# HGRN rows multiplied by the root on GpSimd before they are stored, block decays taken by levels, and the weight splits placed in head 2

## What is computed

```python
hn = rms_norm(h, mix_norm[0])                  # h * rsqrt(mean(h^2) + eps) * gain
u, q_b, f_b, i_b, g_b = split(hn @ w_in_even)
y_a = s5_mixer(u, ...)                         # complex scan over tokens, GELU, GLU
y_b = hgrn2_mixer(q_b, f_b, i_b, g_b, ...)     # 4 heads of 128
h = h + concat(y_a, y_b) @ w_out_even
# in hgrn2_mixer: log_f from f_b, k = (1 - lb) * sigmoid(-f_b), b = cumsum(log_f)
# o = (q * exp(b)) S + causal(q, decay, k) v ; o = rms_norm per head * silu(g_b)
```

## Time and profile before

| | us |
|---|---|
| median of 3 runs | 2599.13 (2596.79 to 2599.51) |
| the profiled execution | 2594.84 |
| its span, first to last instruction | 2593.1 |
| TensorE busy in it | 2458.1 (95%) |
| VectorE busy | 1176.7 (45%) |
| ScalarE busy | 558.3 (22%) |
| GpSimd busy | 822.5 (32%) |
| mean granted TensorE clock | 0.975 of full |

### The profile page before, as it was taken

One profiled execution on the slowest core, in us unless ns is written; L12 is line 12 of the kernel. 1 busy time (PEld: TensorE's weight loads), 2 busy tenths in 40 slices (PEclk: granted clock), 3 DMA queues, 4 the chain that ended last, 5 costly groups with the idle time before them and its releaser, 6 DMA issues.

```text
span 2593.1 us, 32792 instructions
## 1 busy us (share of the span) xinstructions
PE 2458.1 (95%) x13062; PEld 1994.9 (77%) x13062; DVE 1176.7 (45%) x1170; ACT 558.3 (22%) x882; POOL 822.5 (32%) x493
## 2 busy tenths in 40 slices
PE   8999946899999999999996999989999999999997
PEld 6887835688888888888885776668888888888885
DVE  6886388432432422425517355652432332424625
ACT  3111435311001011011212145631001001011215
POOL 3422331132333333333331334552333333333320
PEclk9999967999999999999998999999999999999998
DMA  7372511211111111111213111021111111111211
GB/s 206 104 116 79 159 56 35 98 48 49 49 49 49 49 49 49 49 49 49 65 41 97 41 25 58 24 67 48 49 49 49 49 49 48 46 46 48 63 48 65
DMA packets 249160, 159.65 MB, mean 62 GB/s; under 512 B 32132, under 2 KB 236136, under 8 KB 249064
## 3 DMA queue, kind: packets, MB, share of 16 engines
q1 hardware_dynamic: 233944, 133.92, 18.0%
q10 hardware_dynamic: 15136, 24.58, 3.5%
HBM read 131.81 MB, written 25.49 MB: 61 GB/s over the span
## 4 chain that ended last, share of the span: by engine, by line
PE 85%; DVE 9%; ACT 3%; issue 2%; DMA 1%; POOL 0%; SPq 0%; ACTq 0%; POOLq 0%; DVEq 0%
PE ps L604 70%; PE ps L1086 3%; PE ps L758 2%; PE ps L1118 2%; PE ps L1046 1%; PE ps L1059 1%; PE ps L1070 1%; DVE hg_queries_keys L1861 1%; PE ps L671 1%; PE ps L779 1%; DVE stage L1538 1%; ACT x_hi L1169 1%; DVE hg_block_decay L1847 1%; PE ps L983 1%; DVE residual L2054 1%
## 5 line engine op out<-in xcount | busy, mean ns | idle before, releaser
L459 POOL CAST w_hi<-w_raw 128x1024 fp32r<-128x1024 f32 x198 | 217.9, 1100 | 1499.3 <-PE ps L604 1218.4
L604 PE MATMUL ps<-x_hi,w_hi 128*128 128x512 f32 x1600 | 496.9, 392 | 8.7 <-issue 4.2
L604 PE MATMUL ps<-x_hi,w_lo 128*128 128x512 f32 x1600 | 493.9, 390 | 0.0
L604 PE MATMUL ps<-x_lo,w_hi 128*128 128x512 f32 x1600 | 493.6, 390 | 0.0
L461 POOL TENSOR_TENSOR w_lo<-w_raw,w_hi 128x1024 fp32r<-128x1024 f32 x198 | 484.3, 2446 | 15.9
L604 PE MATMUL ps<-mid_hi,w_hi 128*128 128x512 f32 x1216 | 376.2, 391 | 8.7 <-DVE mid_lo L1913 5.8
L604 PE MATMUL ps<-mid_lo,w_hi 128*128 128x512 f32 x1216 | 375.3, 390 | 0.0
L604 PE MATMUL ps<-mid_hi,w_lo 128*128 128x512 f32 x1216 | 375.3, 390 | 0.0
L604 PEld LDWEIGHTS ps<-x_hi,w_hi 128*128 128x128 f32 x1600 | 300.2, 188 | 75.7 <-issue 9.9
L604 PEld LDWEIGHTS ps<-x_hi,w_lo 128*128 128x128 f32 x1600 | 301.0, 188 | 62.8
L604 PEld LDWEIGHTS ps<-x_lo,w_hi 128*128 128x128 f32 x1600 | 300.9, 188 | 62.9
(11 more groups left out here) (290 smaller groups left out, 2459.4 us busy)
## 6 DMA issues: line engine op xcount, KB each, us to landing
w_raw<-w_mlp_in_in SPq DMA_DIRECT2D x64, 512.0 KB, 4.0
w_raw<-w_mlp_out_in SPq DMA_DIRECT2D x64, 512.0 KB, 4.0
w_raw<-w_in_even_in SPq DMA_DIRECT2D x20, 512.0 KB, 4.2
residual_dram<-residual ACTq DMA_DIRECT2D x2, 4096.0 KB, 12.9
fqig_dram<-stage ACTq DMA_DIRECT2D x16, 512.0 KB, 2.7
w_raw<-w_ple_gate_in SPq DMA_DIRECT2D x16, 512.0 KB, 3.9
x_tokens<-x_in SPq DMA_DIRECT2D x8, 512.0 KB, 7.3
w_raw<-w_out_even_in SPq DMA_DIRECT2D x8, 512.0 KB, 4.2
```

The source lines that it names most:

```text
L459: pool.tensor_copy(WH[:, b, :], RAW[:, b, :]).then_inc(S["w_hi_done"], 1)
L604: ins = pe.matmul(acc[:, h, :], w[:, k, :], x[:, k0 + k, h * HALF:(h + 1) * HALF], start=(k == 0 and w is wh and x is xh), stop=(k == kts ...
```

## The change

GpSimd now multiplies each HGRN row tile by the root as it leaves the projection (`scale_unit`), behind the split of the slab two units later, and SyncE stores it (`spill`), between the loads of slabs. ScalarE only copies. The multiplications of f, q and gate in the heads, the scale per token of the values, its transposes and its column go. `head_load(hd)` waits for the stores of its own rows only. The block decays of head 0 are made one level at a time between its updates, and the clearing of two PSUM banks goes behind update 1. GpSimd splits output slabs 22 and 23 behind `gate_mult(2)` in place of ahead of `gate_mult(0)`.

```diff
 # SyncE
-            with sp.Fori(0, HEADS) as hd:
-                for j, c0 in enumerate((2 * S5W, S5W, 3 * S5W, 4 * S5W)):
-                    load(j % 2, hd * 4 + (4 + j - 1), cols(w_in, bass.ds(hd * P + c0, P)))
+            def head_slab(s):
+                hd, j = divmod(s - SLAB["heads"], 4)
+                c0 = (2 * S5W, S5W, 3 * S5W, 4 * S5W)[j] + hd * P
+                load(s % 2, s - 1, cols(w_in, slice(c0, c0 + P)))
+            def spill(u):
+                sp.wait_ge(S["hg_scaled"], u - 3)
+                sp.dma_start(fqig_dram[(u - 4) * P:(u - 3) * P, :], ST[u % 2][:, :]).then_inc(spilled[u % 2], 16)
...
+            for s in range(4, 8):
+                head_slab(s)
+            for u in range(4, 15):
+                spill(u)
+                head_slab(u + 4)
...
             tile_of_y(0)
-            for s in range(2):
...
-                load(s, 20 + s - 1, src)
-                tile_of_y(s + 1)
+            head_slab(19)
+            spill(15)
+            glu_slab(0)
+            tile_of_y(1)
+            spill(16)
+            glu_slab(1)
+            tile_of_y(2)
+            spill(17)
             tile_of_y(3)
...
+            spill(18)
             load(0, 21, cols(w, slice(0, P)))
-            for b in range(2):
-                sp.wait_ge(spilled[b], 16 * 10)
             sp.wait_ge(S["acc_done"], 20)
             def head_load(hd):
                 p = hd % 2
+                for b in range(2):
+                    sp.wait_ge(spilled[b], 16 * (4 + 2 * hd))
...
             head_load(0)
+            spill(19)
             load(1, 22, cols(w, slice(P, 2 * P)))
 # GpSimd
-            run(4, 4, 16)
-            one(20, 19)
-            one(21, 20)
...
+            def scale_unit(u):
+                if u == 4:
+                    pool.wait_ge(S["rstd_done"], 1)
+                pool.wait_ge(S["acc_free_act"], u - 3)
+                pool.tensor_tensor(ST[u % 2][:, :], ST[u % 2][:, :], RSTD[:, :], ALU.mult).then_inc(S["hg_scaled"], 1)
+            for s in range(4, 22):
+                one(s, s - 1)
+                if s >= 6:
+                    scale_unit(s - 2)
...
-            queries(0)
-            gate_scale(0)
-            one(22, 22)
-            one(23, 24)
             for hd in range(HEADS):
                 gate_mult(hd)
-                if hd < HEADS - 1:
-                    queries(hd + 1)
-                    gate_scale(hd + 1)
+                if hd == 2:
+                    one(22, 22)
+                    one(23, 24)
 # TensorE
-            pe.wait_ge(S["rstd_done"], 1)
-            for n in range(NB):
-                ins = pe.transpose(PS[:, 5, n * GRP:(n + 1) * GRP], RSTD[0:GRP, n * P:(n + 1) * P], ident[0:GRP, 0:GRP])
 # ScalarE
                 fn(ST[b][:, :], flat(ACC[b]), ACT.Copy).then_inc(S["acc_free_act"], 1)
-                act.wait_ge(S["acc_free_act"], u - 3)
-                act.dma_start(fqig_dram[(u - 4) * P:(u - 3) * P, :], ST[b][:, :]).then_inc(spilled[b], 16)
...
-                act.wait_ge(S["hg_z"], u + 1)
+                act.wait_ge(hg_loaded[p][half], 48 * (hd // 2 + 1))
...
-                act.wait_ge(S["hg_g_scaled"], hd + 1)
+                act.wait_ge(hg_g_loaded[hd % 2], 16 * (hd // 2 + 1))
...
-                for c in range(4):
-                    ins = fn(VT[:, half, c * P:(c + 1) * P], PS[:, (2, 3)[half], c * P:(c + 1) * P], ACT.Identity,
-                             scale=rstd_col[:, 4 * half + c:4 * half + c + 1])
-                told(ins, "hg_v_copied")
+                told(fn(VT[:, half, :], PS[:, (2, 3)[half], :], ACT.Copy), "hg_v_copied")
 # VectorE
-            own(dve.tensor_copy(rstd_col[:, :], PS[:, 5, 0:NB * GRP:GRP]))
...
-            def forget_in(hd, half):
-                f = FR[:, hd % 2, half, :]
-                dve.wait_ge(hg_loaded[hd % 2][half], 48 * (hd // 2 + 1))
-                told(tt(f, f, RSTD[:, half * HALF:(half + 1) * HALF], ALU.mult), "hg_z")
...
-            for half in range(2):
-                forget_in(0, half)
             z_low(3)
             near_masks()
             for half in range(2):
                 query_decay(0, half)
-            block_decays(0)
-            dve.wait_ge(S["glu_sig"], 2)
-            for half in range(2):
-                own(dve.memset(PS[:, (6, 7)[half], :], 0.0))
...
                     if hd == 0:
+                        for j in {3: (3, 4, 5, 6)}.get(l, (l,) if l < 3 else ()):
+                            block_decay(0, j)
+                        if l == 1:
+                            dve.wait_ge(S["glu_sig"], 2)
+                            for half in range(2):
+                                own(dve.memset(PS[:, (6, 7)[half], :], 0.0))
                         if l < 4:
                             glu_product(l)
...
-                    if nxt < HEADS and l == (1 if hd == 0 else 2):
-                        for half in range(2):
-                            forget_in(nxt, half)
                     if nxt < HEADS and l == 4:
-                        block_decays(nxt)
+                        for j in range(LEVELS):
+                            block_decay(nxt, j)
```

More of the change, by code:

```diff
@@ L122, in build @@
     eps = small("eps", [P, 1])
-    rstd_col = small("rstd_of_tokens", [P, NB])
     def col(name, i):
@@ L321, in _, with glu_slab @@
                 load(s % 2, s - 1, cols(w_in, slice(s * P, (s + 1) * P)))
-            with sp.Fori(0, HEADS) as hd:
-                for j, c0 in enumerate((2 * S5W, S5W, 3 * S5W, 4 * S5W)):
-                    load(j % 2, hd * 4 + (4 + j - 1), cols(w_in, bass.ds(hd * P + c0, P)))
+            def head_slab(s):
[5 more added lines that the diff above has]
+                sp.dma_start(fqig_dram[(u - 4) * P:(u - 3) * P, :], ST[u % 2][:, :]).then_inc(spilled[u % 2], 16)
+            def glu_slab(s):
+                src = a["s5_w_glu"][0][:, s * 256:(s + 1) * 256].rearrange("(k p) n -> p k n", p=P)
+                load(s, 20 + s - 1, src)
+            for s in range(4, 8):
[3 more added lines that the diff above has]
+                head_slab(u + 4)
             def tile_of_y(k):
@@ L499, in _ @@
                                pattern=[[16, 8], [0, 16]], channel_multiplier=-1).then_inc(S["full_masks"], 1)
-            run(4, 4, 16)
-            one(20, 19)
-            one(21, 20)
-            def queries(hd):
-                for half in range(2):
-                    q = QR[:, hd % 2, half, :]
-                    pool.wait_ge(hg_loaded[hd % 2][half], 48 * (hd // 2 + 1))
-                    pool.tensor_tensor(q, q, RSTD[:, half * HALF:(half + 1) * HALF], ALU.mult).then_inc(S["hg_q_scaled"], 1)
-            def gate_scale(hd):
-                pool.wait_ge(hg_g_loaded[hd % 2], 16 * (hd // 2 + 1))
-                pool.tensor_tensor(G[:, :], G[:, :], RSTD[:, :], ALU.mult).then_inc(S["hg_g_scaled"], 1)
+            def scale_unit(u):
[7 more added lines that the diff above has]
+                    scale_unit(s - 2)
             def gate_mult(hd):
@@ L1830, in query_decay @@
                 dve.wait_ge(S["hg_f_made"], u + 1)
-                dve.wait_ge(S["hg_q_scaled"], u + 1)
+                dve.wait_ge(hg_loaded[p][half], 48 * (hd // 2 + 1))
                 if hd >= 2:
@@ L1841, in blocks, with block_decay @@
                 return TT[:, hd % 2, o:o + (T >> l)]
-            def block_decays(hd):
-                dve.wait_ge(S["hg_f_made"], 2 * hd + 2)
-                for l in range(LEVELS):
-                    pairs = blocks(hd, l).rearrange("p (n two) -> p n two", two=2)
-                    ins = tt(blocks(hd, l + 1), pairs[:, :, 0], pairs[:, :, 1], ALU.mult)
-                    if l < LEVELS - 1:
-                        own(ins)
-                told(ins, "hg_blocks")
+            def block_decay(hd, l):
+                if l == 0:
+                    dve.wait_ge(S["hg_f_made"], 2 * hd + 2)
+                pairs = blocks(hd, l).rearrange("p (n two) -> p n two", two=2)
+                ins = tt(blocks(hd, l + 1), pairs[:, :, 0], pairs[:, :, 1], ALU.mult)
+                if l < LEVELS - 1:
+                    own(ins)
+                else:
+                    told(ins, "hg_blocks")
+                    dve.wait_ge(S["hg_blocks"], hd + 1)
             def update(hd, l):
```

9 lines of the change are left out of this document (3 added, 6 removed).

## The result

The changed kernel takes 2600.94 us (median of 20 runs, 2593.15 to 2608.97), the kernel before, beside it on the same chip, 2597.14 (20 runs, 2587.68 to 2600.3). The medians lie 3.8 us apart. The ratio estimated from all runs of both is 1.0022, its 95% interval 1.0011 to 1.0032: slower by 5.7 us, at the edge of the 0.2% that can be told. The forecast was 1.7 us slower. That the level forecast, 2600.8, is so near to the median measured is partly luck: it was built on a median of three runs, 2599.13, and twenty put the kernel before at 2597.14.

What follows compares the result with a forecast made beforehand. TensorE was taken to bound the kernel, so terms count only where it waits: for VectorE at S5 and in the heads. 15.3 + 1.5 - 10.2 - 3.5 - 1.4 = +1.7 us, 2600.8 us forecast median; range 2590 to 2609.

Steps and rivals of the forecast that it cites:

- A collision costs 2.08 us: Projection with S5: each added GpSimd multiplication that meets a VectorE operation with both operands in SBUF costs VectorE 2.08 us.
- rival (b): Projection: part is hidden, the memset takes one, small waits two, split 16 stays behind L1772; 8.3 us less, 2592.5; chance 0.17.
- The skip addition 9.4 us later: L1724 in the S5 part: seven multiplications, 14.6 us, less the 5.0 wait and 0.2 for the root column's copy.
- Behind it 5.9 us: From L1724 to the S5 output: multiplications of units 11 and 13, a cast and split 16, less 1.9, together +5.9 us.
- rival (a): Locks cost more: multiplications hold VectorE their whole 2.34 us in eleven places, units 4 to 14; 2607 us; chance 0.28.
- rival (c): No delay in S5: VectorE's multiply is not held or slack exists; only the heads' 15.1 us count, 2584; chance 0.05.
- The clock, one fall, 1.5 us: After TensorE's added waits in S5, one fall of the granted clock costs 1.5 us, bounds 0 to 8.5.
- The queues: nothing: Sixteen stores move from ScalarE to SyncE, with slab loads behind them; loads stay early enough and saved issues gain nothing.
- Head 0 shorter by 10.2 us: Head 0: first update 11.3 us earlier, then +2.0 in VectorE's queue and -0.9 for value copies; bounds 8 to 12.
- Head 1, 3.5 us: Head 1: shorter by 3.5 us (2.4 to 4.2), as f multiplications and ScalarE's wait for them go.
- Head 2, 1.4 us: Head 2: shorter by 1.4 us, from a later wait of 1.01 and 0.4; bounds -3 and +3.5.
- Head 3, nothing: Head 3: no next head follows and its multiplication stays, so no change in time.

## Why the prediction was right, and where not

The sign and the mechanism of the main terms were right: slightly slower, since what the root's move takes out of the heads it puts into the S5 queue. The size, 1.7 us against 5.7, was in the range, but below what the runs show. Step by step:

- **A collision costs 2.08 us.** Held: 112.67, 124.52 and 136.38 are each 4.37 us in place of 2.29. Up to the memset VectorE's queue was 12.7 us later than without multiplications (144.82 against 132.1), more than the 10.4 of five collisions; GpSimd's splits came later too and met other operations. Behind it, the memset (3.47 us in all the kernels) let a multiplication pass. On the whole 11.8 us in place of 14.6; rival (b) was right that the memset hides one. That operations with an operand in PSUM keep their time was right, but the row named for it, 184.11, does not show it: GpSimd's subtraction had ended at 182.98. The operation at 217.37 above shows it.
- **The skip addition 9.4 us later.** 8.6 measured, and partly by luck: the multiplications cost 2.8 less than forecast, and 1.8 were lost that no term had (the queue is later by that much even with multiplications of one column). The wait of 5.02 went as forecast. Without multiplications it begins at 165.3, 1.7 earlier than before, although its operands' queue is 1.8 later: the S5 kernel of TensorE and ScalarE comes forward, by ScalarE's saved issues or by the transposes that went, which no run separates. The prediction left that at nothing because VectorE is later in the changed kernel, rightly so there.
- **Behind it 5.9 us.** 5.5 measured (57.7 us from the skip addition to the S5 output in place of 52.2); 5.3 in the kernel with the late multiplications alone. The sum was right, the places only in part. Unit 11's multiplication cost 2.1 as forecast, and split 16 with its cast 2.7 of the 2.9. Unit 13's multiplication and its cast (+2.8 forecast) added 0.8, in the operation ahead of the pair: the pair itself takes 4.57 us, and took 4.56 before under a split, a hold that the prediction did not see. The scans and `turn_back` gave back 0.05 in place of 1.9 (0.6 less for the scans, 0.5 more ahead of them). The two errors of some 2 us, in opposite directions, cancel, which is luck. That the S5 sum came out at 14.1 in place of 15.3 refutes rival (a), which needed 19 at least, and rival (c).
- **The clock, one fall, 1.5 us.** This is the term that was mis-sized. It cost 4.6 us at the S5 output, where 1.5 were forecast: 13.7 us at half clock from 229.9, of which the first 3.4 still lie in the wait. The prediction took the short fall at 479 us as nearest. The one of 17 us in the earlier trace rows was nearer, and the upper bound of 8.5 did hold it. But 17 was not the longest of that trace: the window from 334 to 384 us above stands at 0.52, so the bound was worked out from too short a fall.
- **The queues: nothing.** This step failed. Moved to SyncE, the store of unit 8 waits for its multiplication, is issued 11 us after the copy, among the loads of `s_u`, and TensorE waits 5.0 us for the staging tile behind it. I followed the loads of slabs that stand behind the stores, but not the copy two units on, which needs the store landed. In the profiled execution it costs nothing directly, since VectorE sets the skip addition. What follows it is half clock at 154 us, for 3.4 us in one execution and for 30.7 in two others, of kernels with the same wait. With the store's wait gone the ratio was 0.9995 in place of 1.0022, some 7 us, but not measured side by side, and the pair of traces puts that gain elsewhere, as said above. That the runs of the changed kernel above 2604 us are those with a long fall at 154 fits (12 of 26 runs against none of 11): the long fall makes the skip addition 6.0 to 6.5 us later (181.6 and 182.1), and the slowest run of the kernel with unit 15 first has both it and the short falls behind 1590. It is not shown: no such run of the changed kernel has a trace. The end states waited 3.6 us in place of the 7 or so that the prediction named; the 5.0 us at 150 it did not name.
- **Head 0 shorter by 10.2 us.** From the copy of unit 18 on, the first update is 11.3 us earlier, exactly as worked out, and the rest of head 0 takes 1.8 more where 1.1 was forecast: 9.5. Of head 0's gain the splits' move carries most: counted from unit 18's copy to the sixth update it brings 6.4 us alone, the whole change 9.6. Levels without it bring nothing, and that the two edits together (3.0) need the multiplications of queries and gate out of the way was not seen as a condition.
- **Head 1, 3.5 us.** 2.0 measured in this execution; 4.3 in two others, the changed kernel's second profile and the one with `s_u` later, which lack the 6.8 us of half clock at 393.7 (24.6 us in place of 28.9). In the other variants of the changed kernel it takes 25.8 to 28.0 us. **Head 2, 1.4 us.** 2.3 measured, within its bounds; the last split did meet an update (425.84, 3.20 us). **Head 3, nothing.** 1.9 us longer in the profiled execution: the same work at 0.51 of the clock in place of 0.68. In other executions, of this and of the other kernels, it takes 38.0 to 42.6 us, so this is spread, not the change.

Summed, 14.1 + 4.6 - 9.5 - 2.0 - 2.3 + 1.9 and 0.5 behind the heads are 7.3 us, the 7.1 of the profiled pair within rounding. Against the forecast of 1.7 that is 5.6 more. The errors of the S5 terms (-1.2), head 0 (+0.7), head 1 (+1.5) and head 2 (-0.9) cancel to 0.1; the clock at the S5 output (+3.1), head 3 (+1.9) and the 0.5 make the rest.

Of the signs named ahead, the skip addition (176), the S5 output (234), TensorE's wait (5 to 8 us, now 6.4), the half clock behind it and the decays at 0.2 to 0.7 us each came as said. Level 1 of head 0 came 4.8 us behind level 0 by the starts of the updates and 3.9 by their ends, where within 4 was named. From the S5 output to the last output of head 3 it is 252.5 us in place of 260.0, a gain of 7.5 where 14 was named; of what is missing 3.1 is the clock at the S5 output beyond the 1.5 that the prediction had counted, 1.9 head 3, and 1.3 heads 0 to 2.

## What to carry to other kernels

An operation moved to an idle engine is not free if that engine shares a port or a queue with the late one. Price it by the collision that the trace already shows, then look for what can fill the wait that it makes: here the next unit, with which the kernel was 0.22% faster than before, where the change alone was 0.22% slower (0.57% when measured again). When a store moves from one queue to another, follow two chains: what stands behind it in the new queue, and who reuses the buffer that it reads. When runs of a kernel lie in groups, look where the clock falls in several profiled executions, in the untouched part too, not at the averages; a single profile does not price a change of 0.3%.

## What was unexpected of the hardware

- A wait of TensorE of 5.0 to 6.1 us at 150 us was followed by half clock for 3.4 us (changed kernel), 6.8 (its second profile, and the one kept busy in the later wait) and 30.7 (the kernels with multiplications 4 to 10 only and with unit 15 first), with the same instructions of TensorE ahead of it. The kernels with a wait of at most 1.8 us there had no fall at 154.
- Tiny VectorE operations are held like large ones: an operation over 128x256, 0.43 us else, took 2.50 beside unit 4's multiplication (86.66 us), one over 128x64, 0.23 else, took 2.31 beside unit 5's (97.32 us). The Trainium skill, "SBUF — State Buffer", section "Who interferes with whom", calls the shared port pair "an exclusive lock" between the two engines. The trace agrees as far as VectorE loses nearly the whole of GpSimd's operation: here 2.07 and 2.08 us were lost, a little under the 2.34 us that GpSimd's operation takes when not held, and the memset kept its 3.47 us.
- A store of 512 KB issued in the midst of the eight loads of `s_u` landed 15 us later (138.62 to 153.6); the median of the sixteen stores is 3.3 us.
